# A hybrid attention layer on eight cores: one more tile transposed on PE, cache copies and the sample's attention moved in the tail

## Time and profile before

| | |
|---|---|
| runs of the kernel | 1260.1, 1260.99, 1263.64 us, median 1260.99 |
| profiled execution, slowest core | 1266.89 us, of it 1265.3 between first and last instruction |
| spans of the eight cores | 1258.8 to 1265.3 us |
| mean granted TensorE clock of the cores | 0.977 to 0.980 |
| PE, DVE, ACT, POOL busy | 94%, 58%, 51%, 38% of the span |

### The profile page before, as it was taken

One profiled execution on the slowest core, in us unless ns is written; L12 is line 12 of the kernel. 1 busy time (PEld: TensorE's weight loads), 2 busy tenths in 40 slices (PEclk: granted clock), 3 DMA queues, 4 the chain that ended last, 5 costly groups with the idle time before them and its releaser, 6 DMA issues.

```text
span 1265.3 us, 22145 instructions; the slowest of 8 cores (1258.8 to 1265.3 us)
## 1 busy us (share of the span) xinstructions
PE 1186.2 (94%) x8238; PEld 572.1 (45%) x8238; DVE 729.5 (58%) x1668; ACT 648.0 (51%) x992; POOL 474.5 (38%) x517
## 2 busy tenths in 40 slices
PE   5899799999999999999999999999999999799875
PEld 2454354444444444444444444444444444344432
DVE  2775455555655566556566655555555676466533
ACT  2675353654555555455555555545555555345441
POOL 3743122433444433343443344423334444333500
PEclk9899899999999999999999999999999999899987
DMA  9999423333333333334333333333333344533510
GB/s 182 199 176 168 63 59 75 83 68 61 83 75 70 73 83 78 79 79 83 68 65 79 83 82 63 72 75 78 83 78 72 67 94 91 119 87 95 77 39 8
DMA packets 175307, 108.04 MB, mean 85 GB/s; under 512 B 154080, under 2 KB 159328, under 8 KB 172736
## 3 DMA queue, kind: packets, MB, share of 16 engines
q1 hardware_dynamic: 157664, 72.51, 25.0%
q0 software_dynamic: 17536, 34.12, 17.4%
HBM read 80.56 MB, written 21.50 MB: 81 GB/s over the span
## 4 chain that ended last, share of the span: by engine, by line
PE 76%; DMA 11%; DVE 5%; POOL 3%; issue 2%; SPq 1%; ACT 1%; DVEq 0%; ACTq 0%; POOLq 0%
PE psmm L201 67%; DMA actT<-mbuf 5%; PE pss L201 5%; PE pso L201 4%; DMA actT<-zs 3%; POOL st L191 2%; DMA xb<-xe 1%; SPq L191 1%; DMA kaT<-qkn 1%; DVE xb L191 1%; DVE psmm L191 1%; DVE mbuf L191 1%; DMA identb<-ident 1%; DVE qkn L191 1%; POOL zs L191 1%
## 5 line engine op out<-in xcount | busy, mean ns | idle before, releaser
L201 PE MATMUL psmm<-W_in,xT 128*128 128x512 bf16 (+1 forms) x2848 | 649.1, 371 | 7.7 <-ACT tg L191 7.7
L201 PEld LDWEIGHTS psmm<-W_in,xT 128*128 128x128 bf16 x2848 | 254.1, 98 | 271.3 <-issue 15.7
L191 ACT ACTIVATE ET<-pss 128x1024 bf16<-128x1024 f32 x220 | 224.7, 1021 | 202.7 <-PE pss L201 191.1
L191 POOL TENSOR_TENSOR st<-st,mhalf 128x8 f32<-128x8 f32 (+1 forms) x174 | 225.7, 1309 | 205.3 <-DVE st L191 204.3
L191 POOL TENSOR_TENSOR zs<-ont,zs 128x256 bf16<-128x256 f32 x132 | 89.2, 676 | 249.3 <-DVE ont L191 247.9
L191 ACT ACTIVATE tg<-psmm,st 128x512 bf16<-128x512 f32 x132 | 90.3, 687 | 157.1 <-PE psmm L201 157.1
L191 DVE SCALAR_TENSOR_TENSOR psmm<-tg,psmm 128x512 f32<-128x512 bf16 x66 | 45.5, 691 | 153.0 <-PE psmm L201 152.9
L201 PE MATMUL psmm<-W_out,actT 128*128 128x512 bf16 x528 | 124.1, 387 | 8.4 <-DMA actT<-mbuf 7.6
L201 PE MATMUL psmm<-W_pg,actT 128*128 128x512 bf16 x528 | 123.2, 387 | 5.5 <-DMA actT<-mbuf 4.3
L191 DVE TENSOR_TENSOR qkn<-psmm,st 128x512 bf16<-128x512 f32 (+1 forms) x137 | 82.9, 606 | 77.9 <-POOL st L191 75.8
L191 DVE SCALAR_TENSOR_TENSOR xb<-psmm,xb 128x512 f32<-128x512 f32 x132 | 90.3, 684 | 24.2 <-PE psmm L201 23.9
(11 more groups left out here) (104 smaller groups left out, 1194.4 us busy)
## 6 DMA issues: line engine op xcount, KB each, us to landing
y<-xb SPq DMA_DIRECT2D x32, 512.0 KB, 2.8
xb<-xm SPq DMA_DIRECT2D x29, 512.0 KB, 4.0
W_in<-w_in POOLq DMA_DIRECT2D x10, 1024.0 KB, 28.0
xT<-xmT POOLq DMA_DIRECT2D x28, 256.0 KB, 4.0
xb<-xe POOLq DMA_DIRECT2D x2, 1536.0 KB, 13.5
pT<-pmT POOLq DMA_DIRECT2D x32, 64.0 KB, 2.7
W_out<-w_out POOLq DMA_DIRECT2D x2, 1024.0 KB, 65.4
W_pg<-w_pg POOLq DMA_DIRECT2D x2, 1024.0 KB, 62.5
```

The costliest lines, as they stand in the source:

```text
L191: inst = getattr(e, method)(*[_res(a_) for a_ in args], **{k_: _res(a_) for k_, a_ in kw.items()})
L201: last = getattr(e, m)(*[_res(a_) for a_ in a], **{k_: _res(a_) for k_, a_ in k.items()})
```

## The change

- The fourth main tile (n = 3) no longer uses DMA transposes. The upper limit in the new condition (n < NT = 32) excludes no tile.
- The four cache copies leave `stage_C` for a function of their own. They now read the resource `xb` of the last main tile, so they wait for the last write to it, and they are recorded behind its Z.
- The loop ends two tiles earlier, and the last main tile and the sample are written out: P without merge gates, A and merge gates of the last main tile; P without merge gates, `stage_C` and A of the sample; Z of the last main tile; cache copies; merge gates and Z of the sample.

```diff
--- before.py
+++ after.py
@@ -452,7 +452,7 @@
     tiles.append(dict(kind="sample", vt=SB + 4, x=xs, xT=xsT, p=psT))
     for li, t in enumerate(tiles):
         t["li"] = li
-        t["dmaT"] = t["kind"] == "main" and t["n"] >= 3
+        t["dmaT"] = t["kind"] == "main" and 4 <= t["n"] < NT
 
     cumb = [0.0]
 
@@ -922,11 +922,13 @@
         S.ins("pe", "transpose", trx[:, 0:128], qkn[:, 1024:1152], ident[:], r=["qkn_ka", "ident"], w=[trres])
         S.ins("act", "mul", kaT[:, sl, :], trx[:, 0:128], gcol[:, 0:1], r=[trres, "gcol"], w=[f"kaT{sl}"])
         S.ins("pool", "dma_start", out=va[:, sl, :, 0:64], in_=v3(cvw[:, :], 64), w=[f"va{sl}"], dma=("ccVw", 1))
-        S.ins("sp", "dma_start", out=kws[0:64, :], in_=ckw[64:128, :], dma=("kvc", 1))
-        S.ins("sp", "dma_start", out=vws[0:64, :], in_=cvw[64:128, :], dma=("kvc", 1))
-        S.ins("sp", "dma_start", out=kbs[0:448, :], in_=ckb[64:512, :], dma=("kvc", 1))
-        S.ins("sp", "dma_start", out=vbs[0:448, :], in_=cvb[64:512, :], dma=("kvc", 1))
         yield
+
+    def cache_copies(behind):
+        S.ins("sp", "dma_start", out=kws[0:64, :], in_=ckw[64:128, :], r=behind, dma=("kvc", 1))
+        S.ins("sp", "dma_start", out=vws[0:64, :], in_=cvw[64:128, :], r=behind, dma=("kvc", 1))
+        S.ins("sp", "dma_start", out=kbs[0:448, :], in_=ckb[64:512, :], r=behind, dma=("kvc", 1))
+        S.ins("sp", "dma_start", out=vbs[0:448, :], in_=cvb[64:512, :], r=behind, dma=("kvc", 1))
 
     def tabs_setup():
         S.ins("act", "activation", out=esink, in_=esink, func=AF.Exp, r=["esink"], w=["esink"])
@@ -1039,19 +1041,29 @@
     issue_loadT(tiles[9])
     Z(m[3])
     porder = mains + [samp]
-    for k in range(4, len(porder)):
+    for k in range(4, len(porder) - 2):
         t = porder[k]
         P(t)
         issue_pload(t)
-        if t is samp:
-            S.cur = ("C", t["li"])
-            for _ in stage_C():
-                pass
         A(t)
-        if k + 2 < len(porder):
-            issue_loadT(porder[k + 2], gated(t))
-            issue_load(porder[k + 2], behind=gated(t))
+        issue_loadT(porder[k + 2], gated(t))
+        issue_load(porder[k + 2], behind=gated(t))
         Z(t)
+    t = porder[-2]
+    P(t, "xqz")
+    issue_pload(t)
+    A(t)
+    P(t, "gh")
+    P(samp, "xqz")
+    issue_pload(samp)
+    S.cur = ("C", samp["li"])
+    for _ in stage_C():
+        pass
+    A(samp)
+    Z(t)
+    cache_copies([f"xb{t['li'] % NXB}"])
+    P(samp, "gh")
+    Z(samp)
 
     dma_keys = sorted({o.dma[0] for s_ in S.streams.values() for o in s_ if o.dma is not None})
     sems = {e: es.enter_context(nc.semaphore(f"s_{e}")) for e in Sched.ENGS}
```

## The result

| | before | changed |
|---|---|---|
| runs beside each other, median | 1262.32 us | 1273.28 us |
| lowest to highest | 1260.1 to 1263.65 | 1271.77 to 1276.15 |
| profiled execution | 1266.89 us | 1276.15 us |
| its slowest core's span | 1265.3 us | 1274.6 us |
| spans of the eight cores | 1258.8 to 1265.3 us | 1257.7 to 1274.6 us |

The ratio is 1.0108 with a 95% interval of 1.009 to 1.0126. The forecast was 1231.3 us. In some executions the cores of one die show a lower granted clock and take longer; the medians in this text leave such executions out, and where nearly all of a run's were of that kind (before_lat195, e2_only, e3_only) the time given is the span of the slowest core on a die without it.

The account below looks back on a forecast made before the run. PE was busy 94% of the span, so gains had to come from 79 us of idle PE or lower-clock matmuls. Terms -7.4 - 8.3 - 14.0 = -29.7 us, off the median 1260.99, gave 1231.3 us; range 1223 to 1246.

Parts of the forecast that it names:

- edit 1: Tile 3's transposes moved to PE: removes the hole at 128 us and slow matmuls behind it, net -7.4 us.
- slower, by the scheduler's cycle: Rival: edit in tile 3 puts later tiles into another cycle, W_pg ahead of its actT transpose; 1278 us, chance 0.04.
- the weights were not next: Rival that W_pl's late landing at 134.1 us limits edit 1 to 3 us; 1235.7 us, chance 0.12.
- Edit 2, -8.3: Cache copies moved behind the last main tile's final xb write: removes the hole at 1081 us, -8.3 us.
- The cover: At the end: copies done 12 to 15 us after the y store, the end some 24 us behind it; cost 0.
- Edit 3, -14: Tail: sample's attention ahead of the last tile's dense stage, sample's W_ob done at 1230 not 1244.4, -14 us.
- cache transposes come first, first scores about 1198.5: Step of edit 3 in the tail: cache landed at 1196.7, sample's first scores 14 us earlier.
- the stretched tail: Rival: attention and dense-stage chains in the tail stretch each other, 4 us left of 14; 1241.3 us, chance 0.12.
- settled by itself: Argument against the slower rival: after the one bad tile, with PE waiting 2.18 us at 300.14, the cycle settled again.

Follow-up runs that it names:

- before_lat195: Kernel before with none of the edits, only the scheduler's modelled DMA transpose latency 1.95 instead of 1.9 us; median span 1297 us against 1260.6.
- e2_only: Kernel before with only the four cache copies made to wait for the last main tile's xb; 1249.5 us.
- e3_only: Kernel before with only the sample's attention put ahead of the last main tile's dense stage, cache copies still hoisted; 1248.2 us.
- after_qk_only: Changed kernel, but only q and k of tile 3 are transposed on PE, its actT transposes staying on DMA; 1231.6 us, ratio 0.9762.
- e1_only: Kernel before with only tile 3 transposed on PE, cache copies and tail as before; 1293.35 us, ratio 1.0254.
- e23_only: Changed kernel without the tile 3 edit, which keeps its DMA transposes; cache copies and tail as changed; 1243.3 us, ratio 0.9851.
- after_small_xT: Changed kernel with the loads of transposed x cut to 128 of 1024 columns, same order, output not valid; 1241.7 us, ratio 0.9837.

## Why the prediction was wrong

The step that failed is the one that the sum never wrote down: that tiles 5 to 27 stay 34.1 us each because no edit touches them. They went from 34.8 to 36.7 us each on the slowest core (medians 34.7 and 36.2), 41.8 us in all, as edit 1 put the planner into a cycle with the load of transposed x beside the transposes that W_out waits for. The prediction named the danger as its rival "slower, by the scheduler's cycle", and gave it 0.04.

- *Edit 1, -7.4.* Sized low, if anything. No hole from 128 to 136 us. W_pg's first use is at 134.99 (137 forecast) and W_pl's at 138.44, both without a wait, so the weights were not next. Tile 3's W_ob came 10.6 us earlier, tile 4's 12.2, and 8.0 in after_qk_only. By medians over cores tile 4's is at 235.3 to 236.9 in the three kernels where tile 3's q and k are on PE and the constant is 1.9 (after, e1_only, after_qk_only), and at 244.2 to 246.1 in the four where they are not (before, e2_only, e3_only, e23_only).
- *Edit 2, -8.3.* Held: 9 us. In e23_only the copies stand behind the y store, and the last one, to vbs, lands at 1226.3, 11 us ahead of the sample's store. The cover was there. SP's timeline and the landing:

```profile
1212.64 0.34 SPq L191 DMA_DIRECT2D y<-xb  x1
...
1214.93 0.57 SPq L191 DMA_DIRECT2D vbs<-cvb  x1
...
DMA to landing us min/median/max: 11.4/11.4/11.4
...
1237.51 0.50 SPq L191 DMA_DIRECT2D ys<-xb  x1
```

- *Edit 3, -14.* Direction right, size off: 10 us. The term "cache transposes come first, first scores about 1198.5" took the loads' issue at 1191.69 as given. It hangs on the sample's own keys leaving `qkn`, and in e23_only that is late: the small cache is asked for 0.4 us ahead of the last tile's W_ob, where before it was 10 us ahead. From the end of the last tile's W_pl to the end of the span it takes 31.8 us (forecast 27, before 41). Of the rivals, the stretched tail comes nearest to this, at under half of its price (4 us lost where it had 10).
- *The cycle.* Right in kind: an edit in tile 3 put the later tiles into another cycle, and the time given, 1278, is 5 us from the measured one, by luck, since its place and its count were both off. Wrong in place: not W_pg ahead of its transpose but W_out, with the load of transposed x beside that transpose. Wrong in count too: not 12 tiles at 3.9 us, but all of them at 1.8 us. Against it I set that the cycle "settled by itself" after tile 5. That showed that one cycle existed and held, not that it was the only one the planner could settle in. The trace of before had the evidence: even in the good cycle W_out waited 5.9 us for `actT<-mbuf` from 315 to 1020, and the transposes landed in 2.5 to 3.2 us, in some tiles in 4 to 5, where the model has 1.9. The prediction's 34.1 us is a tile in which PE never waits; with the waits the mean was already 34.7. A plan with less room than the chip takes has little margin for another order.
- *Why edit 1 flips the planner.* With q and k of tile 3 alone on PE the cycle stays (after_qk_only); with its six `actT` transposes as well it flips, and 0.05 us in LAT_T flips it too. That the greedy choice among near-equal starts tips over is argued from these two; which single choice tips was not isolated.

## What to carry to other kernels

When the order is computed greedily over the whole program, an edit is never local: before summing its terms, ask what the order of the untouched loop will be, and treat "the loop stays as it is" as a term with its own chance. Compare the planner's latencies with the landings in the trace; if they are shorter, set them right first (here 1.9 against 2.5 to 4.8, and 3.0 gave 7 to 9 us with no edit and 50 with the change), and only then judge other edits on that base. Where a load is moved on one queue, look for what is in flight on the others.

## What the runs showed of the hardware

- A DMA transpose that is issued within 0.5 us of a 256 KB load on another queue landed in 4.8 us (median of 112 in the changed kernel), and in 2.85 us beside a 32 KB load in the same order (after_small_xT), at a mean DMA share of only 0.34 over the loop. With the 256 KB load issued about 2 us earlier the median was 3.25 us (before), and with it about 2 us later 2.4 us. The mean share says nothing of this; the time between issues and the size of the load do.
- Most of the short waits cost PE's clock nothing. From 315 to 1020 us in the changed kernel, W_out's matmuls ran at 1.2 GHz for a while (634 or 631 ns each and not 379) in 3 tiles, around waits of 1.93, 4.17 and 1.99 us; the mean granted clock of these tiles was 0.95 to 0.96 and that of all others 1.00, one with a wait of 1.98 us among them. In such a tile W_out took 5.3 us and not 3.6; the whole costs some 5 us, where the waits themselves cost 29. This is tile 12 of the changed kernel:

```profile
536.45 5.31 PE L201 MATMUL psmm<-W_out,actT 128*128 128x512 bf16 x16 [4.17 <-DMA actT<-mbuf]
```
